# Order of the high and low matmuls inside a row block, and the row pitch of the tile B, in a two-block fp32 transformer kernel

## Chip, cores and metric

The kernel runs on one core of a Trainium2 chip. The metric is the device time of one execution in microseconds; smaller is better. Engines are named as in the profile: PE is TensorE's matmul stream, PEld its weight loads, DVE is VectorE, ACT is ScalarE, SP the queue that issues the weight transfers.

## Reference: what is computed

Two transformer blocks on 256 tokens of width 2048 in fp32. Block one has differential attention beside a gated MLP with a spatial gate, an output projection, a SwiGLU feed-forward layer of hidden width 5632, and a gated addition of a second input. Block two puts 16 learned tokens ahead of the 256, and has a multi-window pooling branch, a gated three-tap causal convolution, two sigmoid gates, an output projection, a second SwiGLU layer and a final norm. Cut to the part that costs time, it is a row of matrix products `activations @ weight`:

```python
z = rms_norm(h, attn_norm_g) @ w_in                     # 2048 x 5120
h = h + mixed @ w_out                                    # 2048 x 2048
h = h + (silu(f @ ffn_w1) * (f @ ffn_w3)) @ ffn_w2       # 2048 x 5632, twice, and 5632 x 2048
h = h + (p @ pl_w_up) * sigmoid(h @ pl_w_gate)
proj = rms_norm_2(h, norm_mix_g) @ w_in_2                # 2048 x 12288, on 272 tokens
h = h + (g_a * y_a + g_b * y_b) @ w_o
h = h + (silu(gate) * up) @ w_down
```

## The kernel before, in words

**Two parts of each operand.** Every fp32 operand of a large product is held as a high part in the type fp32r (a copy) and a low part (value minus high part). A product is made of three: high weight by high activation, high weight by low activation, low weight by high activation.

**Pieces.** The weights of all products stream through as 940 pieces of 256 rows by 512 columns. SP loads two pieces at a time (1024 KB) into `raw` (a ring of 4). ACT copies a piece into `hi` (L463) and DVE subtracts to make `lo` (L747); `hi` and `lo` are rings of 4 pieces. PE waits for the piece's `lo`, multiplies with it, and counts it in `pieces_used` on its last matmul, which frees the ring slot. ACT and DVE work up to three pieces ahead of PE.

**Order of the pieces.** `schedule()` lists the stages: v, qk, g, u, out, f1_up0, f1_down0, f1_up1, f1_down1, f1_up2, f1_down2, plup, plgate, ga, u2, pool, conv, gbr, cout, wo, f2_up0, f2_down0, and so on to f2_down2. Each is a number of turns of groups of pieces. A group fills four PSUM banks (`b0` to `b0 + 3`); groups alternate between banks 0 to 3 and 4 to 7, so that ACT and DVE empty one half while PE fills the other. A stage with several turns is a loop whose body has fixed addresses.

**Matmuls of a piece.** `piece()` on PE takes the piece's two row blocks (`kk`) in turn, with row `k` of the activation tile `A`, `B` or `PT`. What stands in the row, and which operand is stationary, depends on the stage's layout:

- `halves`: a row is 256 high parts and then 256 low parts. For each of four column blocks `m`, the high weight is stationary and all 512 columns stream (L1203, "H" below), then the low weight is stationary and the 256 high ones stream (L1204, "L" below), both into bank `b0 + m`. `wide_halves`, and the groups "cb" of the stage conv, do the same with 2 x 256 columns out of a row of 2 x 272.
- `token`: the activations are stationary and the weights stream, three matmuls of 512 columns in a row into one bank (L1189 to L1191).
- `packed`: three of 256 columns (L1209 to L1211). `wide` and the rest of conv: three of 272 or of 258 columns into one bank (L1217 to L1219).

A piece in `halves` or `wide_halves` is thus 8 pairs H, L, in the order H0 L0 H1 L1 H2 L2 H3 L3 for each of its two row blocks. Each matmul has its own weight load of 128 columns. 456 pieces do this with A: qk 32, f1_up0, f1_up1, f2_up0 and f2_up1 64 each, f1_up2 and f2_up2 48 each, plgate 32, cout 32, pool 8. 152 do it with B: out 32, f1_down0 to f1_down2 32, 32 and 24, wo 32. 96 do it with B in `wide_halves` (ga, gbr, cb of conv, 32 each). 88 pieces use B in `token` (f2_down0 to f2_down2), 32 A in `token` (v, g).

**Rows in SBUF.** A row of A has 2 x 256 elements (2048 bytes), one of B 2 x 272 (2176 bytes), although 272 columns are used only by block two. `raw`, `hi`, `lo` and A stand ahead of B with sizes that are multiples of 2048 bytes. Behind B stand h, `work` and the other tiles; the tiles of single stages share an arena at the end. `o_head` (a head's attention output) lay in the arena.

Of the kernel before, what the change touches and what calls it, by code (L numbers as in the profile page):

```python
# [23 lines left out]
F32R = mybir.dt.float32r  # L24

P = 128
D = 2048
T = 256
META = 16
TM = META + T  # L30
KT = D // P
GC = 512
MT = GC // P
# [7 lines left out]
LINE = 512  # L41
WINDOWS = (2, 4, 8, 16)
VT0 = META - 2
TV = TM - VT0
RAWS = 4
RING = 4
# [19 lines left out]
def schedule():  # L66
# [3 lines left out]
    def add(*a, **k):  # L70
        s.append(Segment(*a, **k))

    def pair(w, col, row=0):
        return [(w, row, col, 2 * GC), (w, row, col + GC, 2 * GC)]
# [5 lines left out]
    add("u", 1, ["u"] * 2, 8, ("A", "packed", 0), pair("w_in", 3072))  # L80
    add("out", 2, ["res_ffn"] * 2, 8, ("B", "halves", 4), pair("w_out", 0), peel=1)
    n = ffn(add, "f1", 12, ("ffn_w1", 0), ("ffn_w3", 0), "ffn_w2", ["part", "part", "res_gate"], "halves")
# [3 lines left out]
    m, n = n, n + 4  # L86
    add("ga", 2, ["ga"] * 2, 8, ("B", "wide_halves", m), pair("w_in_2", 8192), peel=1)
    add("u2", 1, ["u2"] * 4, 8, ("B", "wide", m), [("w_in_2", 0, GC * g, 0) for g in range(4)])
    add("pool", 1, ["pool"] * 4, 2, ("A", "halves", n), [("pool_w_2", GC * g, 0, 0) for g in range(4)])
    n += 4  # L90
    add("conv", 2, ["cv", "cg", "cb"] * 2, 8, ("B", "conv", m),
        [("w_in_2", 0, c + GC * g, 2 * GC) for g in range(2) for c in (6144, 4096, 2048)])
    add("gbr", 2, ["gbr"] * 2, 8, ("B", "wide_halves", m), pair("w_in_2", 10240))
    add("cout", 2, ["cout"] * 2, 8, ("A", "halves", n), pair("conv_out_w_2", 0))
    n += 4
    add("wo", 2, ["res_ffn2"] * 2, 8, ("B", "halves", n), pair("w_o_2", 0))
    n += 4
# [10 lines left out]
def ffn(add, name, n, gate, up, down, kinds, layout):  # L108

    src = n - 4  # L110
    for c, groups in enumerate((4, 4, 3)):
        first = 4 * GC * c
        add(f"{name}_up{c}", groups, ["gate", "up"], 8, ("A", "halves", src),
            [(gate[0], 0, gate[1] + first, GC), (up[0], 0, up[1] + first, GC)], peel=0 if c else 1)
        add(f"{name}_down{c}", 2, [kinds[c]] * 2, 2 * groups, ("B", layout, n),
            [(down, first, 0, 2 * GC), (down, first, GC, 2 * GC)], peel=2 if c == 2 else 0)
        n += groups
    return n + 4 if kinds[2] == "res_gate" else n
# [79 lines left out]
def bass_two_blocks(nc, ins, out):  # L198
    SEGS, TOTAL = schedule()

    with ExitStack() as ctx:
# [3 lines left out]
        def sb(name, shape, dt=F32):  # L205
            return ctx.enter_context(nc.sbuf_tensor(name, shape, dt))

        def overlay(**shapes):

            with ExitStack() as own:  # L210
                return [own.enter_context(nc.sbuf_tensor(n, s[0], s[1])) if isinstance(s, tuple) else
                        own.enter_context(nc.sbuf_tensor(n, s, F32)) for n, s in shapes.items()]
# [7 lines left out]


        line, _, = overlay(line=[P, HEADS, LINE], pad_line=[P, 1])
        _, ln_rows = overlay(pad_ln=[P, 4 * 2 * TM], ln_rows=[P, 2, 1024])
        _, qk = overlay(pad_qk=[P, 8 * 2 * TM], qk=[P, 16, T])
        _, xtok = overlay(pad_x=[P, 8 * 2 * TM], xtok=[P, 2, D])
        B = sb("B", [P, KT, 2 * TM], F32R)
        h = sb("h", [P, KT, T])
        pb_copy = sb("pb_copy", [P, MT, T])
        work = sb("work", [P, MT, T])
# [10 lines left out]
        metaT = sb("metaT", [P, KT, META])  # L240
        p_in = sb("p_in", [P, 2, T])

        V, U, Gt, bias, wsT, bs_row, probs, probsT, o_head = overlay(
            V=[P, 2, 1024], U=[P, 8, T], Gt=[P, 2, 1024], bias=[P, HEADS, T], wsT=[P, 8, P], bs_row=[P, 8, P],
            probs=[P, 2, 3 * P], probsT=[P, 3 * P], o_head=[P, 2, T])
        _, relb_in, meta_in, vin1, vin2, relb, onehot, lamv, rb = overlay(
            v_skip=[P, 2048 - 8], relb_in=[32, HEADS], meta_in=[META, D], vin1=[V1N, P], vin2=[V2N, P], relb=[32, HEADS, P],
            onehot=[32, LINE], lamv=[P, 4, P], rb=[P, 2, P])
        _, ws_in = overlay(ws_skip=[P, 2 * 1024 + 2048 + 2048 + 1024 + 1024 + 1024], ws_in=[P, 8, P])
        silu_s, UP, PT = overlay(silu_s=[P, MT, T], UP=[P, KT, T], PT=([P, 2, 2 * T], F32R))  # L250
        G1, G2 = overlay(G1=[P, KT, T], G2=[P, KT, T])
        _, win_a, win_b, win_c = overlay(g1_a=[P, KT * T], win_a=[P, MT, TM], win_b=[P, MT, TM], win_c=[P, MT, TM])
        _, cvv, cvg, cvo = overlay(g1_b=[P, KT * T], cvv=[P, MT, TV], cvg=[P, MT, TV], cvo=[P, MT, T])
        _, HT, gfin_row = overlay(silu_b=[P, MT * T], HT=[P, 2, D], gfin_row=[P, D])
        sb("arena", [P, 10900])

        ps = ctx.enter_context(nc.psum_tensor("ps", [P, 8, 512], F32))
        skew = nc.dram_tensor("skewed_lines", [HEADS, P, LINE + 1], F32, kind="Internal").ap()
# [26 lines left out]
        def row_of(r, n):  # L285

            return r.unsqueeze(1).to_broadcast([P, n, r.shape[1]])
# [438 lines left out]
        def _(dve):  # L726
# [43 lines left out]
            def evacuate(kind, G, end, b0, gi, k, more):  # L770
# [109 lines left out]
                elif kind in ("cv", "cg"):  # L880
                    dve.wait_ge(pieces_used, end)
                    to = cvv if kind == "cv" else cvg
                    dve.tensor_tensor(to[:, :, :], ps[:, b0:b0 + 4, 0:TV], row_of(r_row[:, VT0:TM], MT), ALU.mult).then_inc(psum_free, 1)
                    if kind == "cg":
# [262 lines left out]
        def _(pe):  # L1147
# [10 lines left out]
            for k in range(KT):  # L1158
# [5 lines left out]
                for a in range(2):  # L1164
                    last = pe.transpose(ps[:, k // 2, (k % 2) * T + a * P:(k % 2) * T + (a + 1) * P],
                                        xtok[:, a, k * P:(k + 1) * P], ident[:, :])
# [3 lines left out]
            def high(slot, kk, m):  # L1170
                return hi[:, slot % RING, kk, m * P:(m + 1) * P]

            def low(slot, kk, m):
                return lo[:, slot % RING, kk, m * P:(m + 1) * P]

            def piece(seg, g, j, slot, b0, gi):

                buf, layout, _ = seg.reads
                X = {"A": A, "B": B, "PT": PT}[buf]
                for kk in range(2):  # L1180
                    k = 2 * j + kk + (4 * g if seg.name == "pool" else 0)
                    first = j == 0 and kk == 0
                    final = j == seg.pieces - 1 and kk == 1
                    if layout == "token":

                        for a in range(2):
                            Xh, Xl = X[:, k, a * P:(a + 1) * P], X[:, k, T + a * P:T + (a + 1) * P]
                            to = ps[:, b0 + a, :]
                            pe.matmul(to, Xh, hi[:, slot % RING, kk, :], start=first, stop=False)  # L1189
                            pe.matmul(to, Xh, lo[:, slot % RING, kk, :], start=False, stop=False)  # L1190
                            last = pe.matmul(to, Xl, hi[:, slot % RING, kk, :], start=False, stop=final)  # L1191
                        continue
                    for m in range(MT):
                        Wh, Wl = high(slot, kk, m), low(slot, kk, m)
                        if layout in ("halves", "wide_halves") or (layout == "conv" and seg.kinds[g] == "cb"):

                            if layout == "halves":
                                Xh, both, to = X[:, k, 0:T], X[:, k, 0:2 * T], ps[:, b0 + m, :]
                            else:
                                Xh = X[:, k, META:TM]  # L1200
                                both = X[:, k, :].rearrange("p (s t) -> p s t", s=2)[:, :, META:TM]
                                to = ps[:, b0 + m, :].rearrange("p (s t) -> p s t", s=2)
                            pe.matmul(to, Wh, both, start=first, stop=False)  # L1203
                            last = pe.matmul(ps[:, b0 + m, 0:T], Wl, Xh, start=False, stop=final)  # L1204
                        elif layout == "packed":

                            Xh, Xl = X[:, k, 0:T], X[:, k, T:2 * T]
                            to = ps[:, b0 + m // 2, (m % 2) * T:(m % 2 + 1) * T]
                            pe.matmul(to, Wh, Xh, start=first and m % 2 == 0, stop=False, skip_group_check=True)  # L1209
                            pe.matmul(to, Wh, Xl, start=False, stop=False, skip_group_check=True)  # L1210
                            last = pe.matmul(to, Wl, Xh, start=False, stop=final, skip_group_check=True)  # L1211
                        else:

                            t0 = 0 if layout == "wide" else VT0
                            Xh, Xl = X[:, k, t0:TM], X[:, k, TM + t0:2 * TM]
                            to = ps[:, b0 + m, 0:TM - t0]
                            pe.matmul(to, Wh, Xh, start=first, stop=False)  # L1217
                            pe.matmul(to, Wh, Xl, start=False, stop=False)  # L1218
                            last = pe.matmul(to, Wl, Xh, start=False, stop=final)  # L1219
                last.then_inc(pieces_used, 1)  # L1220
# [163 lines left out]
```

## Time and profile before

| what | value |
|---|---|
| median of 3 runs | 2755.94 us (2755.91 to 2756.13) |
| the profiled execution's own time | 2759.01 us |
| its span, first to last instruction | 2757.2 us |
| mean granted TensorE clock | 0.992 |
| PE busy | 2702.3 us (98%), 15696 matmuls |
| DVE busy, ACT busy | 1674.5 us (61%), 1266.6 us (46%) |

PE's busy time overstates its work, since matmuls are pipelined: a row of the trace gives a matmul of 512 columns 0.40 us while the next one starts 0.23 us later. The distance from one start to the next is the number to read, and it is got from rows as the time between first and last start, divided by their count less one.

### The profile page before, as it was taken

To read this page: it belongs to the slowest core of one execution; us is meant where nothing else is said; L and a number is where in the kernel's file an instruction comes from. 1 tells how busy PE (TensorE), PEld (TensorE's weight loads), DVE (VectorE), ACT (ScalarE), POOL (GpSimd) and SP (SyncE) were. 2 spreads that over 40 slices of the span, in tenths; PEclk is the share of its full clock that TensorE was granted. 3 is DMA by queue.
4 is the path that set the end of the run, shared out by engine and by line. 5 is a ranking of instruction groups with operands and counts; after the bars stand their busy time and mean duration, and the time that the engine had idled before them with its cause. 6 is when DMAs were issued, how large, how long until landed. Compare 5 with 4: busy or idle time off the path is not lost.

```text
span 2757.2 us, 40029 instructions
## 1 busy us (share of the span) xinstructions
PE 2702.3 (98%) x15696; PEld 2371.7 (86%) x15696; DVE 1674.5 (61%) x1601; ACT 1266.6 (46%) x1352; POOL 0.8 (0%) x7
## 2 busy tenths in 40 slices
PE   6998999999999999999999999999999999999998
PEld 5887988888888888888999999888888888888886
DVE  4557675655555555687577666556765655564554
ACT  4346554444444444555434434444554434443443
POOL 0000000000000000000000000000000000000000
PEclk9999999999999999999999999999999999999999
DMA  7553555555555555555545555555555555555553
GB/s 233 184 183 117 171 186 185 195 185 183 183 183 186 192 184 193 176 168 191 179 166 184 185 182 184 197 185 194 187 193 189 187 193 183 183 191 190 183 182 123
DMA packets 253102, 504.27 MB, mean 183 GB/s; under 512 B 8018, under 2 KB 10500, under 8 KB 252580
## 3 DMA queue, kind: packets, MB, share of 16 engines
q1 hardware_dynamic: 251348, 498.39, 53.4%
q10 hardware_dynamic: 1632, 4.19, 0.5%
q8 instruction: 83, 1.36, 0.2%
q14 instruction: 39, 0.32, 0.0%
HBM read 499.41 MB, written 3.15 MB: 182 GB/s over the span
## 4 chain that ended last, share of the span: by engine, by line
PE 93%; DVE 4%; ACT 1%; issue 1%; DMA 0%; SPq 0%; ACTq 0%; DVEq 0%
PE ps L1203 46%; PE ps L1204 23%; PE ps L1189 4%; PE ps L1191 4%; PE ps L1190 4%; PE ps L1217 3%; PE ps L1219 3%; PE ps L1218 3%; DVE lo L747 1%; DVE tiny L767 0%; PE ps L1209 0%; PE ps L1210 0%; PE ps L1211 0%; ACT hi L463 0%; DVE work L755 0%
## 5 line engine op out<-in xcount | busy, mean ns | idle before, releaser
L747 DVE TENSOR_TENSOR lo<-raw,hi 128x1024 fp32r<-128x1024 f32 x940 | 1137.6, 1223 | 850.0 <-ACT hi L463 847.4
L463 ACT ACTIVATE hi<-raw 128x1024 fp32r<-128x1024 f32 x940 | 984.5, 1056 | 1012.3 <-PE ps L1204 710.6
L1203 PE MATMUL ps<-A,hi 128*128 128x512 f32 x3648 | 1281.8, 397 | 4.2 <-DVE lo L747 2.6
L1204 PE MATMUL ps<-A,lo 128*128 128x256 f32 x3648 | 1020.6, 280 | 0.0
L1203 PEld LDWEIGHTS ps<-A,hi 128*128 128x128 f32 x3648 | 684.7, 188 | 170.5 <-DVE lo L747 3.8
L1203 PE MATMUL ps<-B,hi 128*128 128x512 f32 x1984 | 698.2, 395 | 1.9 <-DVE lo L747 1.8
L1204 PEld LDWEIGHTS ps<-A,lo 128*128 128x128 f32 x3648 | 688.1, 189 | 0.2
L1204 PE MATMUL ps<-B,lo 128*128 128x256 f32 x1984 | 557.1, 281 | 0.0
L1203 PEld LDWEIGHTS ps<-B,hi 128*128 128x128 f32 x1984 | 372.5, 188 | 91.5 <-DVE lo L747 2.1
L1204 PEld LDWEIGHTS ps<-B,lo 128*128 128x128 f32 x1984 | 373.7, 188 | 0.0
L1217 PE MATMUL ps<-B,hi 128*128 128x258 f32 (+1 forms) x768 | 218.2, 284 | 1.0 <-issue 1.0
L1219 PE MATMUL ps<-B,lo 128*128 128x258 f32 (+1 forms) x768 | 218.6, 285 | 0.0
L1218 PE MATMUL ps<-B,hi 128*128 128x258 f32 (+1 forms) x768 | 218.5, 285 | 0.0
L755 DVE TENSOR_TENSOR work<-ps,pb_copy 128x1024 f32<-128x1024 f32 x92 | 112.6, 1224 | 136.8 <-ACT pb_copy L482 135.0
L482 ACT ACTIVATE pb_copy<-ps 128x1024 f32<-128x1024 f32 x96 | 98.5, 1027 | 159.5 <-PE ps L1204 158.6
L1217 PEld LDWEIGHTS ps<-B,hi 128*128 128x128 f32 x768 | 144.7, 188 | 1.5 <-issue 1.3
L1219 PEld LDWEIGHTS ps<-B,lo 128*128 128x128 f32 x768 | 144.6, 188 | 0.0
L1218 PEld LDWEIGHTS ps<-B,hi 128*128 128x128 f32 x768 | 144.5, 188 | 0.0
L1189 PE MATMUL ps<-hi,B 128*128 128x512 f32 x352 | 138.9, 395 | 0.0
L1191 PE MATMUL ps<-hi,B 128*128 128x512 f32 x352 | 138.4, 393 | 0.0
L1190 PE MATMUL ps<-lo,B 128*128 128x512 f32 x352 | 137.6, 391 | 0.0
L1191 PEld LDWEIGHTS ps<-hi,B 128*128 128x128 f32 x352 | 66.1, 188 | 15.5
(211 smaller groups left out, 1337.6 us busy)
## 6 DMA issues: line engine op xcount, KB each, us to landing
raw<-in_w_in_dram SPq DMA_DIRECT2D x136, 1024.0 KB, 5.0
raw<-in_ffn_w_dram SPq DMA_DIRECT2D x132, 1024.0 KB, 5.0
raw<-in_w_gate_up_dram SPq DMA_DIRECT2D x88, 1024.0 KB, 4.8
raw<-in_w_down_dram SPq DMA_DIRECT2D x44, 1024.0 KB, 5.1
raw<-in_w_out_dram SPq DMA_DIRECT2D x16, 1024.0 KB, 5.1
raw<-in_pl_w_gate_dram SPq DMA_DIRECT2D x16, 1024.0 KB, 5.0
raw<-in_conv_out_w_dram SPq DMA_DIRECT2D x16, 1024.0 KB, 5.1
raw<-in_w_o_dram SPq DMA_DIRECT2D x16, 1024.0 KB, 5.1
```

Of the source, the lines that this page charges most:

```text
L463: act.activation(hi[:, slot % RING], raw[:, raw_slot, 2 * (slot % 2):2 * (slot % 2) + 2, :], ACT.Copy).then_inc(hi_ready, 1)
L482: act.activation(pb_copy[:, :, :], ps[:, b0:b0 + 4, T:2 * T], ACT.Copy).then_inc(copied, 1)
L747: dve.tensor_tensor(lo[:, slot % RING], raw[:, slot // 2 % RAWS, 2 * (slot % 2):2 * (slot % 2) + 2, :], hi[:, slot % RING], ALU.subtract). ...
L755: dve.tensor_tensor(to, ps[:, b0:b0 + 4, 0:T], pb_copy[:, :, :], ALU.add).then_inc(psum_free, 1)
L1189: pe.matmul(to, Xh, hi[:, slot % RING, kk, :], start=first, stop=False)
L1190: pe.matmul(to, Xh, lo[:, slot % RING, kk, :], start=False, stop=False)
L1191: last = pe.matmul(to, Xl, hi[:, slot % RING, kk, :], start=False, stop=final)
L1203: pe.matmul(to, Wh, both, start=first, stop=False)
L1204: last = pe.matmul(ps[:, b0 + m, 0:T], Wl, Xh, start=False, stop=final)
L1217: pe.matmul(to, Wh, Xh, start=first, stop=False)
L1218: pe.matmul(to, Wh, Xl, start=False, stop=False)
L1219: last = pe.matmul(to, Wl, Xh, start=False, stop=final)
```

## The change

Two edits. In `piece()`, for the layouts `halves` and `wide_halves`, the matmul with the low weight of column block m is put behind the one with the high weight of block m + 1. A row block then runs H0 H1 L0 H2 L1 H3 L2 L3 in place of H0 L0 H1 L1 H2 L2 H3 L3. Number, sizes, operands and banks of the matmuls are the same, and the last of a piece is still L3. The other layouts keep their order.

Rows of B get 576 elements (2304 bytes) instead of 544 (2176 bytes); the columns used keep their places at the row's start. The tile grows by 2048 bytes a partition. To make room `o_head` becomes a view of `work`, and the arena shrinks by 532 elements.

```diff
+BROW = 576
...
-        B = sb("B", [P, KT, 2 * TM], F32R)
+        B = sb("B", [P, KT, BROW], F32R)
...
+        o_head = work[:, 0:2, :]
...
-        sb("arena", [P, 10900])
+        sb("arena", [P, 10368])
...
+                        def with_high(m):
+                            to = ps[:, b0 + m, :]
+                            pe.matmul(to if layout == "halves" else to.rearrange("p (s t) -> p s t", s=2), high(slot, kk, m), both,
+                                      start=first, stop=False)
+
+                        def with_low(m):
+                            return pe.matmul(ps[:, b0 + m, 0:T], low(slot, kk, m), Xh, start=False, stop=final)
+
+                        with_high(0)
+                        for m in range(1, MT):
+                            with_high(m)
+                            last = with_low(m - 1)
+                        last = with_low(MT - 1)
+                        continue
...
-                            pe.matmul(to, Wh, both, start=first, stop=False)
-                            last = pe.matmul(ps[:, b0 + m, 0:T], Wl, Xh, start=False, stop=final)
```

## Rows read from the trace of the kernel before

**Rows 1.** The page: span, and busy time of each engine.

```profile
span 2757.2 us, 40029 instructions
...
PE 2702.3 (98%) x15696; PEld 2371.7 (86%) x15696; DVE 1674.5 (61%) x1601; ACT 1266.6 (46%) x1352; POOL 0.8 (0%) x7
```

**Rows 2.** The page: chain that ended last, share by engine and by line.

```profile
PE 93%; DVE 4%; ACT 1%; issue 1%; DMA 0%; SPq 0%; ACTq 0%; DVEq 0%
PE ps L1203 46%; PE ps L1204 23%; PE ps L1189 4%; PE ps L1191 4%; PE ps L1190 4%; PE ps L1217 3%; PE ps L1219 3%; PE ps L1218 3%; DVE lo L747 1%; DVE tiny L767 0%; PE ps L1209 0%; PE ps L1210 0%; PE ps L1211 0%; ACT hi L463 0%; DVE work L755 0%
```

**Rows 3.** The page: groups by line; busy us, mean ns, idle before.

```profile
L747 DVE TENSOR_TENSOR lo<-raw,hi 128x1024 fp32r<-128x1024 f32 x940 | 1137.6, 1223 | 850.0 <-ACT hi L463 847.4
L463 ACT ACTIVATE hi<-raw 128x1024 fp32r<-128x1024 f32 x940 | 984.5, 1056 | 1012.3 <-PE ps L1204 710.6
L1203 PE MATMUL ps<-A,hi 128*128 128x512 f32 x3648 | 1281.8, 397 | 4.2 <-DVE lo L747 2.6
L1204 PE MATMUL ps<-A,lo 128*128 128x256 f32 x3648 | 1020.6, 280 | 0.0
...
L1203 PE MATMUL ps<-B,hi 128*128 128x512 f32 x1984 | 698.2, 395 | 1.9 <-DVE lo L747 1.8
...
L1204 PE MATMUL ps<-B,lo 128*128 128x256 f32 x1984 | 557.1, 281 | 0.0
```

**Rows 4.** Line L1203 in five stretches: count, durations, first to last start.

```profile
L1203 PE MATMUL ps<-A,hi x482: 395/398/403, 669.9 to 839.8; 128*128 128x512 f32 x161
...
L1203 PE MATMUL ps<-A,hi x377: 392/392/395, 429.6 to 560.0; 128*128 128x512 f32 x189
...
L1203 PE MATMUL ps<-A,hi x203: 391/391/391, 1829.8 to 1899.8; 128*128 128x512 f32 x102
...
L1203 PE MATMUL ps<-B,hi x214: 387/396/403, 579.8 to 654.7; 128*128 128x512 f32 x107
...
L1203 PE MATMUL ps<-B,hi x229: 392/396/399, 1739.7 to 1819.7; 128*128 128x512 f32 x115
```

**Rows 5.** The same for lines of the layouts with three matmuls.

```profile
L1190 PE MATMUL ps<-lo,A x16: 389/389/389, 78.6 to 88.8; 128*128 128x512 f32 x16
...
L1190 PE MATMUL ps<-lo,B x94: 389/390/395, 2200.1 to 2264.4; 128*128 128x512 f32 x94
...
L1210 PE MATMUL ps<-A,hi x15: 280/283/283, 297.9 to 302.9; 128*128 128x256 f32 x15
...
L1218 PE MATMUL ps<-B,hi x214: 282/288/291, 1344.7 to 1424.9; 128*128 128x272 f32 x107
...
L1218 PE MATMUL ps<-B,hi x112: 280/284/285, 1460.1 to 1499.9; 128*128 128x258 f32 x112
```

**Rows 6.** Timeline of PE where v ends and qk starts: start us, duration.

```profile
89.03 0.39 PE L1191 MATMUL ps<-hi,A 128*128 128x512 f32 x1
89.26 0.39 PE L1203 MATMUL ps<-A,hi 128*128 128x512 f32 x1
89.49 0.28 PE L1204 MATMUL ps<-A,lo 128*128 128x256 f32 x1
89.60 0.40 PE L1203 MATMUL ps<-A,hi 128*128 128x512 f32 x1
89.83 0.28 PE L1204 MATMUL ps<-A,lo 128*128 128x256 f32 x1
89.95 0.40 PE L1203 MATMUL ps<-A,hi 128*128 128x512 f32 x1
90.19 0.28 PE L1204 MATMUL ps<-A,lo 128*128 128x256 f32 x1
90.31 0.40 PE L1203 MATMUL ps<-A,hi 128*128 128x512 f32 x1
```

**Rows 7.** Waits of PE, longest first: us in total, times, longest.

```profile
PE ps L1315 <- ACT probsT L683: 10.7, 3, 6.8
```

More of the change, by code:

```diff
@@ L222, in bass_two_blocks @@
         line, _, = overlay(line=[P, HEADS, LINE], pad_line=[P, 1])
-        _, ln_rows = overlay(pad_ln=[P, 4 * 2 * TM], ln_rows=[P, 2, 1024])
-        _, qk = overlay(pad_qk=[P, 8 * 2 * TM], qk=[P, 16, T])
-        _, xtok = overlay(pad_x=[P, 8 * 2 * TM], xtok=[P, 2, D])
-        B = sb("B", [P, KT, 2 * TM], F32R)
+        _, ln_rows = overlay(pad_ln=[P, 4 * BROW], ln_rows=[P, 2, 1024])
+        _, qk = overlay(pad_qk=[P, 8 * BROW], qk=[P, 16, T])
+        _, xtok = overlay(pad_x=[P, 8 * BROW], xtok=[P, 2, D])
+        B = sb("B", [P, KT, BROW], F32R)
         h = sb("h", [P, KT, T])
@@ L241, in bass_two_blocks @@
         p_in = sb("p_in", [P, 2, T])
-        V, U, Gt, bias, wsT, bs_row, probs, probsT, o_head = overlay(
+        V, U, Gt, bias, wsT, bs_row, probs, probsT = overlay(
             V=[P, 2, 1024], U=[P, 8, T], Gt=[P, 2, 1024], bias=[P, HEADS, T], wsT=[P, 8, P], bs_row=[P, 8, P],
-            probs=[P, 2, 3 * P], probsT=[P, 3 * P], o_head=[P, 2, T])
+            probs=[P, 2, 3 * P], probsT=[P, 3 * P])
+        o_head = work[:, 0:2, :]
         _, relb_in, meta_in, vin1, vin2, relb, onehot, lamv, rb = overlay(
@@ L1192, in piece @@
                         continue
+                    if layout in ("halves", "wide_halves") or (layout == "conv" and seg.kinds[g] == "cb"):
+                        if layout == "halves":
+                            Xh, both = X[:, k, 0:T], X[:, k, 0:2 * T]
+                        else:
+                            Xh = X[:, k, META:TM]
+                            both = X[:, k, 0:2 * TM].rearrange("p (s t) -> p s t", s=2)[:, :, META:TM]
+                        def with_high(m):
[10 more added lines that the diff above has]
+                        continue
                     for m in range(MT):
                         Wh, Wl = high(slot, kk, m), low(slot, kk, m)
[L1195 to L1202, printed above, removed]
-                            pe.matmul(to, Wh, both, start=first, stop=False)
-                            last = pe.matmul(ps[:, b0 + m, 0:T], Wl, Xh, start=False, stop=final)
-                        elif layout == "packed":
+                        if layout == "packed":
                             Xh, Xl = X[:, k, 0:T], X[:, k, T:2 * T]
```

## Prediction, made before the changed kernel was run

> **What bounds the kernel now.** I read the page first, then the chain, then the starts of single matmuls. The busy line puts PE at 2702.3 of 2757.2 us, with DVE at 61% and ACT at 46% [rows 1], and the chain that ended last runs for 93% through PE, 69% of the span in the two lines of the changed layouts [rows 2]. PE stands idle 54.9 us in all (2757.2 - 2702.3); the largest item is 10.7 us in attention [rows 7], which the change doesn't touch. So time can come only from the distance between one matmul's start and the next, and the view for that is a line's first and last start over a stretch in which PE never pauses.
>
> The reader should see in [rows 4] that the same code has several prices. Start to start of H, which is one pair H + L, is:
>
> - A in f1_up1: (839.8 - 669.9) / 481 = 353.2 ns, "dear". Four more stages were read and give 353.2 to 353.5: qk, f1_up2, f2_up1, f2_up2.
> - A in f1_up0: 130.4 / 376 = 346.8; in cout: 70.0 / 202 = 346.5. "Cheap".
> - B in `halves` (f1_down0): 74.9 / 213 = 351.6; f1_down1 gives the same.
> - B in `wide_halves` (gbr): 80.0 / 228 = 350.9.
>
> 768 columns at the full 2.4 GHz would be 320 ns; so a pair carries 27 to 33 ns of something else. The layouts with three matmuls [rows 5] show its size for one: 10.2 / 15 / 3 = 226.7 ns for 512 columns with A (213.3 + 13.4), 5.0 / 14 / 3 = 119 for 256 (106.7 + 12), 125.5 for 272 and 119.5 for 258 (12 each). So about 13.3 ns per matmul is a floor that no row goes under on average, and 226.7 + 120 = 346.7 is exactly the cheap pair. The dear pair has 6.6 ns more, B in `halves` 5, and B in `token` has 64.3 / 93 / 3 = 230.5 against A's 226.7, 3.8 more. Where the tile's rows are 2048 bytes apart the price is either the floor or the dear one, by stage; where they are 2176 apart it is neither. I read this as a pattern of starts into which PE's two reads (the streaming operand and the next weights) fall: it depends on where the operands lie and on what went before, and it persists.
>
> **The change part by part.** Counts: 704 of the 940 pieces are changed, 8 pairs each: 5632 pairs (3648 with A and 1984 with B [rows 3], and 32 of plup besides), or 1408 row blocks of four pairs. They are 256 dear A pieces (the five stages above, 512 blocks), the other 200 A pieces, taken as cheap (400 blocks; the rows cover f1_up0 and cout), 152 B pieces (304 blocks), 96 wide ones (192 blocks). A block costs now 4 x 353.3 = 1413.2 ns dear, 4 x 346.7 = 1386.8 cheap, 4 x 351.7 = 1406.8 in B, 4 x 350.8 = 1403.2 wide.
>
> *The new order.* A block has still four H, four L and eight weight loads; of the eight steps from a start to the next, three are H to L, three L to H, one H to H, one L to L. No weight load becomes shorter or rarer: L's still stand behind 512 columns in three cases, and four loads stand behind 256 columns as before. H to H is what `token` does: 226.7. L to L is what `packed` does: 120. For the three pairs in between I have one place where two H-like matmuls precede: [rows 6], where v's run of 512-column matmuls goes over into qk. From 89.26 to 90.31 three pairs take 1.05 us, 350 each: the first is 340 (0.23 + 0.11), the second 350, the third 360, and from there on the stage is dear. A new block breaks off after three pairs. So the estimate is 226.7 + 1050 + 120 = 1397 ns. Bounds: below, all steps at the floor, 4 x 346.7 = 1386.8; above, the three pairs dear, 346.7 + 3 x 353.3 = 1406.6. Outside these: H to H at 240 and L to L at 124 (0.24 is the longest step from an H in [rows 6]; 4 ns over the floor for L as for B in `token`), with dear pairs, 1424.
>
> I take 1397, since it is the one sequence that the trace shows. Sum over the blocks: dear A 512 x -16 = -8.3 us; cheap A 400 x +10 = +4.1; B 304 x -10 = -3.0; wide 192 x -6 = -1.2. Together -8.4 us.
>
> *Is there something in the accumulator?* If L waited because H just before it wrote the same bank, the new order would remove that wait. The `token` rows speak against it: three matmuls follow each other in one bank and then comes another bank, and the mean over all steps is still the floor, 226.7 [rows 5]. I price it at nothing.
>
> *Rows of 2304 bytes.* 2304 is 9 x 256, and A's 2048 is 8 x 256; 2176 is 8.5 x 256, so B's odd rows now lie half way. If the pattern depends on this, B behaves like A. In `token`, which keeps its order, 88 pieces x 12 matmuls x (230.5 - 226.7) = -4.0 us. Bounds: 0, and -4.0. I take all of it, as A in `token` shows no other price. For B in `halves` it is already in the block prices. `wide` and the rest of conv are at 12 ns per matmul, under the floor that I take, so there is nothing to win; +-1.5 us for 96 pieces x 24 matmuls at 0.6 ns.
>
> Here the Trainium skill speaks against the change. The page "SBUF — State Buffer" (section "Who interferes with whom") gives PE two independent read ports, one for the moving operand and one for weight loads, and says that PE never waits on anyone; by that neither pitch nor order would matter and the time would stay at 2756, against the 2743.5 below. By that rule, the trace disagrees as far as it goes. The rows themselves say that the same instructions take 346.8 or 353.2 ns in stretches without a pause. The page "TensorE: Matmul & The Clock Gate" (section "Back-to-back issue gap") has N / 2.4 + 2.5 ns per matmul, an estimate of 325 ns for a pair in any order; the rows show 346.5 to 353.5.
>
> *Costs hidden elsewhere.* `o_head` in `work`: same instructions and sizes; in stages g and u nothing else writes `work`, so no new wait. The longer rows of B cost ACT and DVE nothing, whose instructions keep their sizes. A piece's last matmul stays L3, so the ring slots come free as now. DVE needs 1.22 us and ACT 1.06 us for a piece [rows 3] out of PE's 2.8, so a faster PE finds its pieces ready; if that cover were gone, PE would wait for L747 before each piece, which now sums to 4.4 us ahead of L1203 (2.6 + 1.8).
>
> Sum: -8.4 - 4.0 = -12.4 us against the profiled execution's span of 2757.2. That execution took 2759.01 us, of which 1.8 lie around the span, and is 3.1 above the median of the runs. From the median: 2755.9 - 12.4 = 2743.5 us.
>
> **The rivals.**
>
> 1. *All steps at the floor.* For: `token`, `packed` and two A stages sit there, `token` and `packed` from any start, and every block now has an H H and an L L that could pull the pattern back. Against: qk comes straight from such a run and turns dear at once [rows 6]. Sum: dear A 512 x -26.4 = -13.5; cheap 0; B 304 x -20 = -6.1; wide 192 x -16.4 = -3.1; token -4.0: -26.7 us, 2729 us.
> 2. *Nothing changes that can be measured.* Either (a) pitch and order don't matter and all stays as it is, 2756, or (b) all three pairs of a block are dear beside a cheap H H and L L, 1406.6 ns: dear A -3.4, cheap A +7.9, B 0, wide +0.7, token -4.0, +1.2 in all, 2757 us. For (b): the dear price is what most A stages hold. Against (a): the stages with two prices for one code. Case (a) is the rule of the Trainium skill's page "SBUF — State Buffer" quoted above.
> 3. *Slower: the pattern never settles.* With every block's H H and L L at 240 and 124 ns and dear pairs, 1424 ns: dear A +5.5, cheap A +14.9, B +5.2, wide +4.0, token -4.0: +25.6 us, 2781 us. It decides above 1410 ns a block (break-even of the whole is 1406 with the token gain), that is from about 3 ns over the floor in H H plus L L beside dear pairs. For: f1_up0, f2_up0 and cout are at the floor now and can only lose by a new order. Against: no such price for H H with aligned rows in [rows 5].
> 4. *The accumulator matters after all.* A pair at the 340 ns that [rows 6] shows once would give 1360 a block, about 1408 x 43 = -61 us, 2695. The `token` rows exclude it nearly.
>
> **How the numbers follow.** Chances: the forecast 0.36, rival 1 0.24, rival 2 0.18 (0.05 for a, 0.13 for b), rival 3 0.20, rival 4 0.02. 0.2% of this time is 5.5 us, about what a measurement of the kernel can tell from no change. Faster holds the forecast and rivals 1 and 4: 0.62; same 0.18; slower 0.20. The forecast's own range is 2737 to 2750. The range for 8 in 10 goes down past rival 1 to 2727 and up past rival 2 into the mild half of rival 3, 2765. The predicted time is 2743.5 us.
>
> **What would show it right or wrong.** In the changed kernel a block's eight starts in f1_up1 should span 1387 to 1407 ns (H to H near 227, L to L near 120), the same in f1_up0 and in f1_down0, since A and B now have one alignment and one order; f1_up0 should be slower than now, f1_up1 faster. L1190's line in f2_down should stand at 227 instead of 230.5 per matmul. PE's idle time stays near 55 us and DVE's waits stay on ACT. I am wrong if f1_up1's block is above 1413, if H H costs more than 235, or if `token` with B keeps 230.5: then alignment to 256 bytes isn't what the rows differ by.

## The result: slower by 0.29%, and the profile after

The changed kernel takes 2762.92 us (median of 11 runs), the kernel before 2755.59 in the same comparison. Of each kernel's 11 runs one took 6852 us and is left out of the ratio; the others of the changed kernel lie between 2762.3 and 2764.2. The ratio is 1.0029, 95% interval 1.0021 to 1.0036; the medians are 7.3 us apart, so the change makes the kernel slower, by more than the 0.2% that the prediction took as the least difference that can be told. I had forecast 2743.5 us in a range of 2727 to 2765; the time is inside the range, on the wrong side of the kernel before.

The page after, to be read against [rows 1] and [rows 2]:

```profile
span 2760.7 us, 40029 instructions
...
PE 2706.1 (98%) x15696; PEld 2373.0 (86%) x15696; DVE 1674.2 (61%) x1601; ACT 1266.7 (46%) x1352; POOL 0.8 (0%) x7
...
PE 92%; DVE 5%; ACT 2%; issue 1%; DMA 0%; SPq 0%; ACTq 0%; DVEq 0%
```

PE is idle for 54.6 us (2760.7 - 2706.1; before 54.9), DVE and ACT are as busy as they were. PE as a whole waits no longer; the time is in the distances between matmuls. Line L1204 (H, L1203 before) in the five stretches of [rows 4], then L1192 (L1190 before) with B as in [rows 5]:

```profile
L1204 PE MATMUL ps<-A,hi x482: 395/396/403, 669.8 to 839.8; 128*128 128x512 f32 x161
...
L1204 PE MATMUL ps<-A,hi x369: 395/396/403, 429.9 to 559.9; 128*128 128x512 f32 x185
...
L1204 PE MATMUL ps<-A,hi x199: 395/400/403, 1829.7 to 1899.7; 128*128 128x512 f32 x199
...
L1204 PE MATMUL ps<-B,hi x214: 395/398/403, 579.7 to 655.0; 128*128 128x512 f32 x107
...
L1204 PE MATMUL ps<-B,hi x230: 392/394/398, 1739.7 to 1819.9; 128*128 128x512 f32 x115
...
L1192 PE MATMUL ps<-lo,B x96: 389/389/389, 2200.0 to 2264.6; 128*128 128x512 f32 x96
```

Per pair, with before in brackets: f1_up1 170.0 / 481 = 353.4 ns (353.2), f1_up0 130.0 / 368 = 353.3 (346.8), cout 70.0 / 198 = 353.5 (346.5), B in `halves` 75.3 / 213 = 353.5 (351.6), B in `wide_halves` 80.2 / 229 = 350.2 (350.9), B in `token` 64.6 / 95 / 3 = 226.7 per matmul (230.5). The granted clock is 1.00 in all these stretches, before and after. The reader should see that A now has one price, the dear one, where it had two, and that B has joined it. The first starts of the row blocks in the trace say it more finely: 1413.3 ns a block in all A pieces and B pieces in `halves` once a stage has settled and where no pause touches it, 1400 in `wide_halves`.

The two profiled executions are only 3.5 us apart (2757.2 and 2760.7). Some 4 us of the loss are made good in two stretches with next to no changed matmul: qk starts 2.4 us sooner in the second one, with a granted clock of 0.90 against 0.86 in the 70 us before it, and the 15.2 us from f1_down2 to plgate, at a granted clock of 0.89, became 13.8 at 1.00.

One block of f1_up1 in PE's timeline (two equal matmuls in a row share a line, "x2"):

```profile
721.86 0.63 PE L1204 MATMUL ps<-A,hi 128*128 128x512 f32 x2
722.33 0.28 PE L1208 MATMUL ps<-A,lo 128*128 128x256 f32 x1
722.45 0.40 PE L1204 MATMUL ps<-A,hi 128*128 128x512 f32 x1
722.68 0.28 PE L1208 MATMUL ps<-A,lo 128*128 128x256 f32 x1
722.80 0.40 PE L1204 MATMUL ps<-A,hi 128*128 128x512 f32 x1
723.04 0.40 PE L1208 MATMUL ps<-A,lo 128*128 128x256 f32 x2
723.28 0.63 PE L1204 MATMUL ps<-A,hi 128*128 128x512 f32 x2
```

H0 to H1 to L0 takes 0.47 us, L0 to H2 0.12, H2 to L1 0.23, L1 to H3 0.12, H3 to L2 0.24, L2 to L3 to the next H0 0.24: 1.42 at this resolution. The starts in the trace, averaged over the blocks from 670 to 830 us, are finer: H0 to H1 235.8 ns, the three pairs behind it 233.3 + 113.3, 232.5 + 117.5 and 240.9 + 120.0 (the last is L2 to L3), and L3 to the next H0 120.0.

The first block of qk, straight behind v, is another one (the rows after it are the second block and the start of the third):

```profile
86.85 0.61 PE L1204 MATMUL ps<-A,hi 128*128 128x512 f32 x2
87.30 0.28 PE L1208 MATMUL ps<-A,lo 128*128 128x256 f32 x1
...
88.24 0.63 PE L1204 MATMUL ps<-A,hi 128*128 128x512 f32 x2
88.71 0.28 PE L1208 MATMUL ps<-A,lo 128*128 128x256 f32 x1
...
89.66 0.63 PE L1204 MATMUL ps<-A,hi 128*128 128x512 f32 x2
```

It has H0 H1 L0 in 0.45 us and lasts 1.39 us (1397 ns by the trace, which is the forecast price), the second one 0.47 and 1.42. In this stage only the first block begins afresh. f2_up1 and f2_up2, which stand behind `token` too, begin in the same way.

A loss that I had not priced is in conv, whose `wide`-like groups keep their order but read B at the new pitch. L1218 before and L1231 after, both in the second pair of groups of a turn:

```profile
L1218 PE MATMUL ps<-B,hi x121: 278/283/288, 1528.8 to 1571.9; 128*128 128x258 f32 x121
```

```profile
L1231 PE MATMUL ps<-B,hi x121: 288/288/288, 1530.0 to 1574.0; 128*128 128x258 f32 x121
```

43.1 / 120 / 3 = 119.7 ns per matmul became 44.0 / 120 / 3 = 122.2. conv has four such places of 16 pieces. Two of them rose like this, 32 pieces x 24 x 2.5 ns = 1.9 us; a third fell from about 120.5 to 119.7, -0.3 us. Together conv lost some 1.6 us.

### The profile page after: what moved, and what is told of

The parts are those of the page before. It is cut to its first block, busy times and chain, and to the rows that moved or that the text cites. A ratio compares the mean times of both kernels' runs of the same rounds, so it can differ in the third digit from the quotient of the medians.

```text
span 2760.7 us, 40029 instructions
## 1 busy us (share of the span) xinstructions
PE 2706.1 (98%) x15696; PEld 2373.0 (86%) x15696; DVE 1674.2 (61%) x1601; ACT 1266.7 (46%) x1352; POOL 0.8 (0%) x7
## 4 chain that ended last, share of the span: by engine, by line
PE 92%; DVE 5%; ACT 2%; issue 1%; DMA 0%; SPq 0%; ACTq 0%; DVEq 0%
PE ps L1204 46%; PE ps L1208 23%; PE ps L1191 4%; PE ps L1193 4%; PE ps L1192 4%; PE ps L1231 3%; PE ps L1230 3%; PE ps L1232 3%; DVE lo L749 1%; DVE tiny L769 1%; ACT hi L465 0%; DVE work L757 0%; PE ps L1243 0%; PE ps L1223 0%; PE ps L1222 0%
## 5 line engine op out<-in xcount | busy, mean ns | idle before, releaser
L1204 PE MATMUL ps<-A,hi 128*128 128x512 f32 x3648 | 1218.8, 399 | 3.7 <-DVE lo L749 2.3
L1208 PE MATMUL ps<-A,lo 128*128 128x256 f32 x3648 | 876.5, 281 | 0.0
L1204 PEld LDWEIGHTS ps<-A,hi 128*128 128x128 f32 x3648 | 623.8, 188 | 84.0 <-DVE lo L749 2.9
L1204 PE MATMUL ps<-B,hi 128*128 128x512 f32 x1984 | 661.7, 397 | 2.0 <-DVE lo L749 1.8
L1208 PE MATMUL ps<-B,lo 128*128 128x256 f32 x1984 | 475.5, 281 | 0.0
L1204 PEld LDWEIGHTS ps<-B,hi 128*128 128x128 f32 x1984 | 338.5, 188 | 45.6 <-DVE lo L749 1.7
L1231 PE MATMUL ps<-B,hi 128*128 128x258 f32 (+1 forms) x768 | 219.5, 286 | 0.0
L1230 PEld LDWEIGHTS ps<-B,hi 128*128 128x128 f32 x768 | 145.8, 190 | 1.2 <-issue 1.2
L1231 PEld LDWEIGHTS ps<-B,hi 128*128 128x128 f32 x768 | 144.2, 188 | 0.0
L1192 PE MATMUL ps<-lo,B 128*128 128x512 f32 x352 | 136.9, 389 | 0.0
```

Source lines behind the costliest of these rows:

```text
L1204: pe.matmul(to if layout == "halves" else to.rearrange("p (s t) -> p s t", s=2), high(slot, kk, m), both, start=first, stop=False)
L1208: return pe.matmul(ps[:, b0 + m, 0:T], low(slot, kk, m), Xh, start=False, stop=final)
```

## The experiments

All kernels but the three streams compute the reference. In each the ratio is to the kernel before on the same chip; the chips differ by about 1 us in that kernel's median (2754.0 to 2755.6), so small differences between runs of different chips say little. All these kernels, the streams apart, keep `o_head` in `work`. Prices of row blocks are differences of starts in the trace.

### e1_pitch: the row pitch alone

```diff
-                        with_high(0)
-                        for m in range(1, MT):
-                            with_high(m)
-                            last = with_low(m - 1)
-                        last = with_low(MT - 1)
+                        for m in range(MT):
+                            with_high(m)
+                            last = with_low(m)
```

> Only the rows of B become 576 elements; the order stays H0 L0 H1 L1. Theory 'persisting pattern': the price of a pair is a state (346.7 or 353.3 ns) that is handed on between stages whose rows lie alike, and only a pause or an odd pitch sets it anew. Then qk and out stay dear (B's block 1413 ns), the pause in f1_up0 sets it cheap (1387 ns a block) and it stays cheap through f1_down0, f1_up1, f1_down1, f1_up2 and f1_down2: 112 pieces x -53 ns = -6.0 us and 88 x -40 = -3.5; cout hands cheap on to wo, 32 x -40 = -1.3; B in the token layout falls from 230.5 to 226.7 ns a matmul, -4.1. About -14.5 us, 2741 us. Rival 'pitch is the culprit': aligned rows of B drive all into the dear price, f1_up0 and cout too, and the run is as slow as the changed kernel, 2763 us. Rival 'nothing persists': A stages stay as in the kernel before, B dear, +2 - 4 = -2 us.

2743.06 us against 2755.18, ratio 0.9956 (0.9943 to 0.9970): 12 us faster than before and 20 us faster than the changed kernel. L1204 here is H again, in f1_up1, f1_down0 and qk:

```profile
L1204 PE MATMUL ps<-A,hi x483: 392/395/395, 669.7 to 836.7; 128*128 128x512 f32 x161
...
L1204 PE MATMUL ps<-B,hi x217: 392/392/395, 579.9 to 654.8; 128*128 128x512 f32 x109
...
L1204 PE MATMUL ps<-A,hi x199: 395/398/403, 104.9 to 174.9; 128*128 128x512 f32 x199
```

167.0 / 482 = 346.5 ns in f1_up1, 74.9 / 216 = 346.8 with B, 70.0 / 198 = 353.5 in qk. Where stages follow each other directly, the state is handed on as the theory said: dear from out into f1_up0, cheap from the pause in f1_up0's eighth piece to the end of f1_down2 (1387 ns a block for 700 us), and cheap from cout through wo into f2_up0. It is dear in qk, in out (between the two stand g and u, with other layouts and pauses), and in f2_up1 and f2_up2, which stand behind a `token` stage. Both rivals fall: A is not dear everywhere, and f1_up1 changed without an edit of its own. Two things were not foreseen: plgate begins dear here after the pauses of plup, and f2_up0 stays cheap through its own pauses, so a pause can change the state but need not.

### e2_order: the order alone

```diff
-BROW = 576
+BROW = 544
```

(against the changed kernel)

> Only the order changes (H0 H1 L0 H2 L1 H3 L2 L3); rows of B stay at 544. Theory 'the order itself has one price': A stands at 1413 ns a block in every stage, f1_up0 and cout too (+9.1 us), B in token stays at 230.5, B in halves somewhere within 1400 to 1420; 2763 to 2768 us. Rival 'pitch is the culprit': A keeps its two prices and the total stays within 3 us of the kernel before.

2759.12 us, ratio 1.0013 (1.0004 to 1.0023).

```profile
L1204 PE MATMUL ps<-A,hi x482: 395/396/403, 669.7 to 839.7; 128*128 128x512 f32 x161
...
L1204 PE MATMUL ps<-B,hi x216: 388/392/398, 580.0 to 655.0; 128*128 128x512 f32 x108
```

A is dear, 170.0 / 481 = 353.4, and in the trace so in every stage, f1_up0 and cout too. B at the odd pitch has a price of its own, 75.0 / 215 = 348.8 a pair, under the 351.6 that the old order has there. So the total is 4 to 9 us under what I had expected for it. The rival "pitch is the culprit" falls: A is dear at the old pitch. Order and pitch don't add up: the pitch gives the old order 12 us and costs the new one 4 (2762.9 - 2759.1). By the two traces the 4 us are B in `halves` from 1397 to 1413 ns a block (+5.0), `wide_halves` from 1393 to 1400 (+1.3), conv and u2 (+1.4) and `token` (-4.1).

### e3_4h4l and e6_two: other orders

```diff
-                        with_high(0)
-                        for m in range(1, MT):
-                            with_high(m)
-                            last = with_low(m - 1)
-                        last = with_low(MT - 1)
+                        for m in range(MT):
+                            with_high(m)
+                        for m in range(MT):
+                            last = with_low(m)
```

is e3_4h4l. e6_two runs H0 H1 L0 L1 H2 H3 L2 L3 (also against the changed kernel, pitch 576):

```diff
+                        for m in range(0, MT, 2):
+                            with_high(m)
+                            with_high(m + 1)
+                            with_low(m)
+                            last = with_low(m + 1)
```

> Changed kernel with the order H0 H1 H2 H3 L0 L1 L2 L3. If each change from H to L and back costs something and runs of one kind are at the floor (226.7 and 120), a block has one change each way instead of four and should come to 1387 to 1400 ns: 704 pieces x up to -54 ns against the changed kernel, 2725 to 2743 us. If the surplus hangs on each weight load and its phase instead, the block is again at 1413 or above, 2763 us or more. If the accumulator mattered (L right behind H in one bank), this order, with four matmuls between, would be below the floor, under 2725.

> Rows of B at 576 with the order H0 H1 L0 L1 H2 H3 L2 L3. The stream gave 1393 ns a block for it from every marker. If the stream stands for the kernel: 704 pieces at 2787 ns, against the changed kernel 2827: -28 us, 2735 us. If the kernel's pauses and ring addresses matter beyond that, up to 1413, 2763 us.

e3_4h4l: 2751.79 us, 0.9989 (0.9980 to 0.9998). e6_two: 2741.45, 0.9949 (0.9936 to 0.9963). The H lines in f1_up1, of e3_4h4l and of e6_two:

```profile
L1204 PE MATMUL ps<-A,hi x480: 387/396/398, 669.8 to 837.5; 128*128 128x512 f32 x160
```

```profile
L1204 PE MATMUL ps<-A,hi x479: 393/396/398, 669.7 to 836.2; 128*128 128x512 f32 x160
```

The trace gives 1403.3 ns a block for e3_4h4l and 1393.3 for e6_two, in all stages of the layout `halves` (but f2_up0 of e3_4h4l, 1400 behind a pause). Fewer changes between H and L do not make the block cheap: 4H 4L has one each way and is dearer than HH LL with two. That falls against the first theory of e3_4h4l's expectation; the second, 1413 or above, missed too. The third falls as well: this order puts three matmuls (not four, as the expectation has it) between the H and the L of a bank, and the block is not below the floor. e6_two came out 6 us above its expectation, nearly all of it from `wide_halves`: it was priced with the others as falling from 2827 to 2787 ns a piece, but stood at 2800 in the changed kernel and rose to 2813, which makes 5 us over 96 pieces.

### m1_streams: PE alone

A stream of matmuls on data at rest; ACT and DVE are done before it starts, and the share of DMA is 0.00. Each matmul overwrites its bank instead of adding to it. It leaves out everything else of the kernel. L68 is H, L71 is L.

```python
for n in STARTS:            # 32, 96, 160, 224 columns
    marker(n)               # one matmul of n columns
    for i in range(REPS):   # six row blocks
        ...                 # H and L in the case's order
```

> Not the computation of the reference: output is zeros. A stream of matmuls on data at rest in SBUF, 18 cases one after the other, each four times with six row blocks after a marker matmul of 32, 96, 160, 224 columns, nothing else running. Cases 1 to 6: orders H L, the new one, 4H 4L, HH LL, H alone, L alone, aligned. 7 to 12: order H L with weights or the streaming operand moved by 64 or 128 bytes. 13 to 18: H alone, L alone, the new order and 4H 4L with moved weights. Theory 'the surplus is made by PE's own two reads': the prices of the kernel come back with no other engine at work: 1387 or 1413 ns a block in case 1, depending on the marker; 1413 in case 2; 226.7 and 120 ns in cases 5 and 6; and moved addresses change them. Rival 'other engines or transfers disturb PE': all cases are near 320 to 325 ns a pair here, and the order makes no difference.

Window of the first case, busy time of the engines, and share and GB/s of DMA at the end:

```profile
30.00:52.00 22.00, 22.00 (x128) 19.23 (x127) 0.00 (x0) 0.00 (x0) 0.00 (x0) 1.00 0.00 1
```

In the timeline, first H of the second and of the sixth row block, order H L, behind the marker of 32 columns (first two rows) and of 160 (last two):

```profile
29.11 0.39 PE L68 MATMUL ps<-X,W 128*128 128x512 f32 x1
...
34.66 0.39 PE L68 MATMUL ps<-X,W 128*128 128x512 f32 x1
...
46.00 0.40 PE L68 MATMUL ps<-X,W 128*128 128x512 f32 x1
...
51.65 0.40 PE L68 MATMUL ps<-X,W 128*128 128x512 f32 x1
```

5.55 / 4 = 1387 ns and 5.65 / 4 = 1412: the kernel's cheap and dear price from the same instructions and addresses, told apart by one matmul in front. The new order behind its last marker, H0 and H1 of the second and sixth block; then H alone and L alone, 48 in a row:

```profile
88.87 0.63 PE L68 MATMUL ps<-X,W 128*128 128x512 f32 x2
...
94.52 0.63 PE L68 MATMUL ps<-X,W 128*128 128x512 f32 x2
...
197.11 11.08 PE L68 MATMUL ps<-X,W 128*128 128x512 f32 x48
208.03 0.18 PE L65 MATMUL ps<-X,W 128*128 128x32 f32 x1
208.06 6.00 PE L71 MATMUL ps<-X,W 128*128 128x256 f32 x48
```

5.65 / 4 = 1412 for the new order. It settles there from each of the four markers; from the marker of 32 columns two blocks of 1398 and 1407 come first. The rows of 48 last 11.08 and 6.00 us with the tail of the last, 226.7 and 120 ns from start to start in the trace. The settled price of a row block, got from the starts in the trace, for each marker:

| case | 32 | 96 | 160 | 224 |
|---|---|---|---|---|
| H L, aligned | 1387 | 1387 | 1413 | 1413 |
| new order, aligned | 1413 | 1413 | 1413 | 1413 |
| 4H 4L | 1403 | 1403 | 1403 | 1403 |
| HH LL | 1393 | 1393 | 1393 | 1393 |
| H L, low weights at 64 bytes | 1387 | 1387 | 1387 | 1387 |
| H L, low weights at 128 bytes | 1400 | 1400 | 1387 | 1387 |
| H L, all weights at 64 bytes | 1413 | 1413 | 1413 | 1413 |
| new order, all weights at 64 bytes | 1407 | 1407 | 1407 | 1407 |
| new order, all weights at 128 bytes | 1400 | 1400 | 1400 | 1400 |

4H 4L alternates between 1400 and 1406. The row blocks of the cases left out of the table settle on average between 1396 and 1414: the streaming operand moved by 64 or 128 bytes, and all weights moved by 128 bytes in the old order or in 4H 4L. The kernel's prices for A come back without another engine or a transfer. The rival is out.

### m2_shifts: addresses and layouts

```python
case(OLD, wl=64)               # low weights 256 bytes on; then x=64, then both weights
case(OLD, wl=8)                # and 16, 24, 48; the same for wh, high weights
token(wl=16)                   # the layouts of the kernel
narrow(0, rows=32)             # 512 columns streamed over weights of 32 columns
```

The same stream with other offsets, in elements of 4 bytes.

> Not the computation of the reference: output is zeros. 34 more cases of matmul streams on data at rest, four marker lengths each (32, 160, 200, 224 columns), five row blocks. If the price depends on addresses modulo 256 bytes, the first three cases (low weights, streaming operand, all weights moved by 256 bytes) repeat the aligned ones: 1387 or 1413 ns by the marker. Low weights moved by 32, 64, 96, 192 bytes: the theory of two colliding reads of PE expects 1387 whatever the marker for 64 again, and no rule for the others. Orders with low weights at 64 bytes, the layouts token, packed, wide and conv with and without it, and row pitch 544 follow. Last three: weights of 128, 64, 32 columns in front of 512 streamed ones: if the 13.3 ns over 213.3 come from the weight load, they shrink with it; if they are fixed per matmul, 226.7 ns stays.

Moving low weights, streaming operand or all weights by 256 bytes repeats the aligned case to the nanosecond, 1387 or 1413 by the marker. Low weights at 32 or 64 bytes give 1387 from every marker, at 96 from three of four, at 192 they give 1400 to 1409. High weights at 64 or 192 bytes with aligned low ones give 1360 from three markers and 1400 from one: less than 1387. `token` with streamed low weights at 64 bytes rises from 226.7 to about 232 per matmul, `packed` falls from 120 to 117.8. The same 64 bytes that make the old order cheap from every marker make HH LL dear, 1413 from three markers and 1400 from one (1393 aligned): a shift is good for one order and not for another. With the layout `wide_halves` at pitch 576 the old order gives about 1404, HH LL 1407 and the new order 1400, which is what e1_pitch, e6_two and the changed kernel have there.

Weights of 128, 64 and 32 columns in front of 512 streamed ones, 40 in a row each:

```profile
941.70 9.27 PE L117 MATMUL ps<-X,W 128*128 128x512 f32 x40
950.81 0.18 PE L64 MATMUL ps<-X,W 128*128 128x32 f32 x1
...
978.72 9.36 PE L117 MATMUL ps<-X,W 128*64 128x512 f32 x40
...
997.31 9.41 PE L117 MATMUL ps<-X,W 128*32 128x512 f32 x40
```

A load of a quarter of the columns takes nothing off the surplus; the row is even 0.14 us longer (9.41 against 9.27), that is 231.7 ns a matmul against 226.7 (230.0 with 64 columns). The loads themselves do get shorter in the trace, 188, 134 and 109 ns. So the surplus isn't in proportion to the length of the weight load.

### e4_lo64 and e5_new_lo64: the low weights moved in the kernel

```diff
         B = sb("B", [P, KT, BROW], F32R)
+        sb("lo_before", [P, 16])
+        lo = sb("lo", [P, RING, 2, GC], F32R)
```

(and `lo` taken away where it stood, so that all tiles behind it start 64 bytes later too); e4_lo64 on e1_pitch, e5_new_lo64 on the changed kernel.

> Order of the kernel before, rows of B at 576, and the ring of low weights moved by 64 bytes (16 elements) off the 256-byte grid. Theory 'two reads of PE collide by address and phase': as in the stream with low weights moved by 64 bytes, a block costs 1387 ns in every stage whatever happened before; against the run with the pitch alone: qk, f2_up1, f2_up2 and parts of out and plgate lose 53 ns a piece, some 200 pieces, -10 us; the token layout streams these low parts, so it may leave 226.7. About 2732 us. Rival 'the state is set by the other engines': prices as in the run with the pitch alone, 2743 us.

> The changed kernel (new order, 576) with the low weights moved by 64 bytes. If the new order is dear by itself whatever the addresses, it stays at 1413 ns a block and 2763 us; if its price too comes from where the two reads fall, the block moves (with all weights moved by 64 bytes the stream gave 1407), up to -27 ns a block, 2745 to 2763 us.

e4_lo64: 2737.01 us, 0.9936 (0.9922 to 0.9950), the lowest median found, 26 us under the changed kernel's. The intervals of e6_two and e1_pitch overlap it, so which of the three is fastest is not shown by the times. e5_new_lo64: 2760.16, 1.0019 (1.0010 to 1.0029). H (L1205 in these) in f1_up1 and f1_down0 of e4_lo64:

```profile
L1205 PE MATMUL ps<-A,hi x476: 390/392/393, 669.9 to 834.6; 128*128 128x512 f32 x159
...
L1205 PE MATMUL ps<-B,hi x218: 391/392/393, 579.8 to 655.0; 128*128 128x512 f32 x109
```

and in f1_up1 of e5_new_lo64:

```profile
L1205 PE MATMUL ps<-A,hi x484: 395/398/398, 669.8 to 839.8; 128*128 128x512 f32 x162
```

164.7 / 475 = 346.7 and 75.2 / 217 = 346.5 ns: cheap in all stages of the layout `halves`, qk and f2_up1 too, whatever came before (`wide_halves` stands at 1400 in ga and at 1387 in gbr). The rival "other engines" falls. The 5 us over my estimate come mainly from the `token` stages, which stream these weights: 2720 ns a piece became some 2785. The new order stays above: 170.0 / 483 = 352.0, 1406.7 a block, as in the stream; so its price too depends on the addresses.

### e7_hi64 and m3_starts: the high weights moved

```diff
         B = sb("B", [P, KT, BROW], F32R)
+        sb("hi_before", [P, 16])
+        hi = sb("hi", [P, RING, 2, GC], F32R)
```

(against e1_pitch)

> Order of the kernel before, rows of B at 576, low weights aligned, the ring of high weights moved by 64 bytes. In the stream this gave 1360 ns a block (340 a pair, under the 1387 that I called the floor) from three of four markers and 1400 from the fourth. If the kernel falls into the first state: 608 pieces at 2720 ns against some 2800 now, -48 us, less what the token layout, which streams these weights, loses: 2700 to 2715 us. If it falls into the second, 2800 ns a piece: 2750 to 2755 us. Rival 'the floor is a fixed cost per matmul': not below 2773 ns a piece anywhere.

```diff
-STARTS = (32, 160, 200, 224)
+STARTS = tuple(range(16, 272, 16))
```

(against m2_shifts, with other cases)

> Not the computation of the reference: output is zeros. Twelve cases of streams, each from 16 marker lengths (16 to 256 columns in steps of 16), four row blocks each. If the state of the aligned order H L is set by the phase at which it starts, the 16 markers split into a group at 1387 and one at 1413 ns a block, in a regular pattern of the marker's length, with high weights at 64 bytes into 1360 and 1400, while the new order gives 1413 from all 16. If it were chance, the split would show no pattern.

e7_hi64 (the shift of e4_lo64 applied to `hi`, `lo` aligned): 2743.20 us, 0.9958 (0.9944 to 0.9971). H in f1_up1, then in f2_up2:

```profile
L1205 PE MATMUL ps<-A,hi x484: 393/394/396, 669.7 to 838.8; 128*128 128x512 f32 x162
...
L1205 PE MATMUL ps<-A,hi x296: 389/389/389, 2549.7 to 2650.0; 128*128 128x512 f32 x148
```

169.1 / 483 = 350.1 ns, and 100.3 / 295 = 340.0. The 340 ns pair, under what I had called a floor, is real and lasts through f2_up2, f2_up0 and a part of plgate; most stages fall into the 1400 state, some into 1413, and `token` rises to 233. So the total lies between the two that I had given, and the rival "the floor is a fixed cost per matmul" falls: 2720 ns a piece in f2_up2. The state decides, and I didn't control it.

m3_starts, 16 markers from 16 to 256 columns: the aligned order H L settled at 1387 from nine (16, 32, 48, 64, 96, 128, 144, 208, 256) and at 1413 from seven. With high weights at 64 bytes it settled at 1360 from seven, 1400 from six and 1413 from three. The new order settled at 1413 from 15; from the marker of 256 columns its third and fourth block stood at 1406 and 1407, most likely not yet settled, since out in the changed kernel begins with 1398, 1406 and 1407 and then stands at 1413. The split is not the regular pattern that I had expected. For the aligned order H L the markers of 32, 96, 160 and 224 columns gave the same states as in m1_streams, so there it is hardly chance. With high weights at 64 bytes the marker of 32 gave 1400 in m2_shifts and 1360 here; the streams ahead of this marker differ, and so does the chip, and each stream ran once. Which of these changed the state stays open.

## Why the prediction was wrong, point by point

**The bound** was read rightly: PE's start-to-start distances, with idle time, ACT and DVE unmoved. **That the price is a persisting pattern** set by addresses and by what went before was right, and m1_streams shows it with PE alone.

**The step that failed** is the price of a new block, 226.7 + 1050 + 120 = 1397 ns. I took H to H from a layout that runs H's only, and the three pairs from the one place where a stage begins after such a run [rows 6], as if each block began afresh ("a new block breaks off after three pairs"). But a block begins where the one before ended. A price of 1397 or 1398 is met only in the first block behind another layout or a pause (in qk, out, f2_up1 and f2_up2, say); after one to three blocks it is 1413.3. Of the 16 ns, 9 are H to H (235.8 against 226.7) and 7.5 are the three pairs (1057.5 against 1050); only L to L was right at 120. These are the steps of the dear state: the old order in f1_up1 runs in cycles of three pairs, 236 + 113, 233 + 117 and 241 + 120 ns, and a new block is such a cycle with one more H step of 233 and one more L step of 120. In m1_streams it settles there from every marker. My upper case "three pairs dear, H H and L L at the floor", 1406.6, failed in H to H. Of my signs of being wrong, H to H above 235 and the block above 1413 came, both by a hair; `token` at 230.5 didn't. What happened is nearest to rival 3, which was said to decide above 1410 ns a block. But its reason was wrong: the pattern does settle, in the dear state, and H H and L L cost less than its 240 and 124.

**The terms of the sum.**

| term | forecast, us | by the trace after, us |
|---|---|---|
| dear A, 256 pieces | -8.3 | 0 |
| cheap A, 200 pieces | +4.1 | +8.7 (some 163 were cheap, x 53 ns) |
| B in `halves`, 152 | -3.0 | +2.0 (2813.3 to 2826.7 a piece) |
| `wide_halves`, 96 | -1.2 | -0.6 (2806.7 to 2800) |
| B in `token`, 88 | -4.0 | -4.1 (2766.7 to 2720) |
| conv and u2 | 0 +- 1.5 | +1.7 |
| sum | -12.4 | +7.7 |

The medians say +7.3. The `token` term was right to 0.1 us, and so was the reason for it, that rows 2304 bytes apart behave like rows 2048 apart: m2_shifts finds a shift of 256 bytes without effect. "Taken as cheap" was too broad for A: f1_up0 up to its pause (16.9 us for 48 pairs from 394.9 us on, 352 ns each) and plgate behind one (12.0 us for 34 pairs from 1197.9 us on, 353) were dear before. In place of "`wide` and conv: nothing to win, +-1.5", conv lost 1.6. The "floor that no row goes under", 13.3 ns per matmul, was none: the rows of 272 and 258 columns [rows 5] had 12 ns already, and e7_hi64 has pairs of 340 ns. Rival 4's 2695 us leaves out the -4.0 of `token` that the other sums hold; with it the sum is 2691.

**B.** I priced B's gain only inside the new order. The two edits don't add up (e1_pitch -12, e2_order +4, both +7.3), and the one worth having was the pitch under the old order.

**The accumulator** was priced at nothing, and the runs show nothing of it: e3_4h4l, with three matmuls between H and L of a bank, stands at 1403 ns a block, above the old order's cheap state with H and L of a bank side by side, and m1_streams, whose matmuls overwrite and never add, has the kernel's prices (1387, 1413, 1403 and 1393) for the four orders.

**The rule that neither matters.** By the section "Who interferes with whom" of the Trainium skill's page "SBUF — State Buffer", PE never waits on anyone and its two read ports are independent. m1_streams agrees with the first half as far as it goes: no other engine is needed for the prices of A. Against what I would draw from the second half, both order and addresses change the time, 1360 to 1427 ns for the same eight matmuls in the three streams. The prediction's 325 ns for a pair come from the section "Back-to-back issue gap" of the Trainium skill's page "TensorE: Matmul & The Clock Gate", which gives that formula for isolated matmuls, without a budget for weight loads; no H L pair here comes down to it, 340.0 ns is the least on average.

**Left open.** What in PE makes the surplus. That the streaming read and the next weight read collide fits the dependence on addresses modulo 256 bytes and on the start phase; but weights of 32 columns, whose loads are shorter, do not shorten it. The collision is argued, not shown. Nor did I find what rule maps a start phase to a state.

## What to carry to other kernels

Where PE is the bound and a line of one shape shows two start-to-start prices in stretches without a pause, the order, the start phase and the operands' addresses (here modulo 256 bytes) are the thing to vary, and a stream of matmuls alone on the chip prices a candidate in one run before the kernel is touched: it gave the block prices of e4_lo64 and e6_two in `halves` before they ran, though not which of its states e7_hi64 would fall into. Don't build the price of a new sequence from steps seen in other sequences; the pattern must settle first. And test edits apart: here one was a gain of 12 us that the other turned into a loss of 7.

## What the runs showed of the hardware that was not expected

- Identical matmuls on identical addresses hold one of two or three prices, in the kernel over hundreds of microseconds, 346.7 or 353.3 ns a pair (340, 350 or 353.3 with high weights at 64 bytes), at a granted clock of 1.00; one matmul of another length in front can switch them, and so can a pause (it did in f1_up0 of e1_pitch, not in f2_up0).
- A matmul with its own weight load took 226.7 ns for 512 columns and 120 for 256 (213.3 and 106.7 at 2.4 GHz) whenever a stream was uniform and aligned and its weights had 128 columns; with 64 and 32 columns of weights it was 230.0 and 231.7 ns for 512. With low weights at 64 bytes L alone went down to 113.3 ns from two of the four markers.
- Moving one operand of a stream by 64 bytes moves a row block between 1360 and 1427 ns (the latter is HH LL with high weights at 64 bytes, in m3_starts); in the order H L, the one tried, 256 bytes move nothing.
